# Per-head norms summed on all channels, the power on 256 columns, and the transposed update on all four quarters of TensorE

## The reference, cut to what matters

```python
kk = (k * k_k).astype(jnp.float32).reshape(B, S, H, N)
kk = kk / jnp.maximum(jnp.sqrt(jnp.sum(kk * kk, axis=-1, keepdims=True)), 1e-12)
...
y = wkv7_scan(rh, decay, kh, vh, -kk, kk * ah)
mu = jnp.mean(y, axis=-1, keepdims=True)
var = jnp.mean(jnp.square(y - mu), axis=-1, keepdims=True)
yn = ((y - mu) * lax.rsqrt(var + RWKV_GN_EPS)).reshape(B, S, RW)
```

## Time and profile before

| | |
|---|---|
| median of 3 runs | 1863.61 us (1862.12 to 1864.73) |
| the profiled execution | 1873.29 us, of which the span of its instructions 1871.5 us |
| TensorE matmul busy | 1844.7 us (99%) |
| TensorE weight load busy | 1570.5 us (84%) |
| VectorE, ScalarE, GpSimd busy | 1181.7, 1029.5, 89.4 us |
| mean granted TensorE clock | 0.992 |

### The profile page before, as it was taken

The page is one execution under the profiler, slowest core; times in us unless marked ns, Lnnn a source line. Parts: engine busy times, 40 slices in busy tenths (PEclk is TensorE's granted clock), DMA queues, the critical chain, the costliest instruction groups (busy, mean ns, idle before and its releaser), DMA issues.

```text
span 1871.5 us, 31118 instructions
## 1 busy us (share of the span) xinstructions
PE 1844.7 (99%) x12714; PEld 1570.5 (84%) x12714; DVE 1181.7 (63%) x2432; ACT 1029.5 (55%) x2127; POOL 89.4 (5%) x186
## 2 busy tenths in 40 slices
PE   8999999999999999999999999999999999999998
PEld 7888888888787888888888887888888888878887
DVE  5666545767655567665766664667566767566565
ACT  5565555644433555555655665556455656655554
POOL 0000000211210000010001000000000000000000
PEclk9999999999979999999999999999999999999999
DMA  6555443222214456535652333556355623334552
GB/s 245 181 204 234 160 156 113 103 86 73 97 53 161 136 191 227 201 113 186 238 194 85 133 134 113 189 211 231 112 184 209 235 98 133 136 113 169 202 186 107
DMA packets 42718, 296.30 MB, mean 158 GB/s; under 512 B 4832, under 2 KB 4960, under 8 KB 10576
## 3 DMA queue, kind: packets, MB, share of 16 engines
q1 hardware_dynamic: 41184, 288.48, 43.1%
q0 software_dynamic: 1392, 5.83, 0.9%
HBM read 293.25 MB, written 1.05 MB: 157 GB/s over the span
## 4 chain that ended last, share of the span: by engine, by line
PE 91%; DVE 4%; ACT 3%; DMA 1%; issue 1%; POOL 1%; SPq 0%; POOLq 0%; DVEq 0%; ACTq 0%
PE PS L1865 22%; PE PS L1807 16%; PE PS L1809 15%; PE PS L1808 15%; PE PS L1867 11%; PE PS L1816 1%; PE PS L2108 1%; DVE wlo L2742 1%; PE PS L2310 1%; PE PS L1842 1%; PE PS L2222 1%; PE PS L2089 1%; PE PS L2274 1%; PE PS L2266 1%; PE PS L2101 1%
## 5 line engine op out<-in xcount | busy, mean ns | idle before, releaser
L2742 DVE TENSOR_TENSOR wlo<-raw,whi 128x512 fp32r<-128x512 f32 (+5 forms) x788 | 612.4, 823 | 191.4 <-ACT whi L2353 184.6
L1865 PE MATMUL PS<-xhl,whi 128*128 128x512 f32 x1728 | 612.6, 398 | 0.0
L2353 ACT ACTIVATE whi<-raw 128x512 fp32r<-128x512 f32 (+5 forms) x788 | 531.6, 731 | 140.1 <-PE PS L1809 140.0
L1867 PE MATMUL PS<-xhl,wlo 128*128 128x256 f32 x1728 | 484.7, 280 | 0.0
L1865 PEld LDWEIGHTS PS<-xhl,whi 128*128 128x128 f32 x1728 | 324.6, 188 | 78.9
L1867 PEld LDWEIGHTS PS<-xhl,wlo 128*128 128x128 f32 x1728 | 326.2, 189 | 2.1
L1807 PE MATMUL PS<-whi,yh 128*128 128x512 f32 (+2 forms) x572 | 225.8, 395 | 0.4 <-DVE yl L3127 0.3
L1808 PE MATMUL PS<-wlo,yh 128*128 128x512 f32 (+2 forms) x572 | 222.4, 389 | 0.0
L1809 PE MATMUL PS<-whi,yl 128*128 128x512 f32 (+2 forms) x572 | 222.4, 389 | 0.0
L1807 PE MATMUL PS<-whi,xhl 128*128 128x512 f32 (+4 forms) x480 | 191.4, 399 | 0.3 <-DVE wlo L2742 0.3
L2827 DVE TENSOR_TENSOR arena<-arena,PS 128x256 f32<-128x256 f32 x216 | 90.3, 418 | 159.1 <-ACT arena L2423 159.1
(11 more groups left out here) (268 smaller groups left out, 2405.4 us busy)
## 6 DMA issues: line engine op xcount, KB each, us to landing
raw<-wall SPq DMA_DIRECT2D x249, 1024.0 KB, 4.8
raw<-wall SPq DMA_DIRECT2D x12, 768.0 KB, 4.2
raw<-wall SPq DMA_DIRECT2D x8, 968.0 KB, 4.7
raw<-wall SPq DMA_DIRECT2D x4, 896.0 KB, 4.5
arena<-ebias POOLq DMA_DIRECT2D x2, 768.0 KB, 5.1
raw<-wall SPq DMA_DIRECT2D x2, 720.0 KB, 4.2
raw<-wall SPq DMA_DIRECT2D x2, 640.0 KB, 3.7
X<-x SPq DMA_DIRECT2D x2, 512.0 KB, 6.1
```

The costliest lines, as they stand in the source:

```text
L1865: e.matmul(b, hi[:, c0:c0 + 128], xhl[:, k, :, :].rearrange("p a t -> p (a t)"), start=(k == 0), stop=False, skip_group_check=True)
L1867: p = e.matmul(b[:, 0:256], lo[:, c0:c0 + 128], xh[:, k, :], start=False, stop=(k == 7), skip_group_check=True)
L2353: e.activation(whi[slot_of(i)][:, c].bitcast(F32R), raw[i % 3][:, c], copy).then_inc(*M.sig("whi", ("split", i, q)))
L2742: e.tensor_tensor(wlo[slot_of(i)][:, c], raw[i % 3][:, c], whi[slot_of(i)][:, c].bitcast(F32), ALU.subtract).then_inc(*M.sig("wlo", *[("ha ...
```

## The change

The two norms are summed with the block matrix `bones` (ones where two channels are of one head) as the stationary operand and the squares moving. Every channel of a head then holds its head's sum for every row: 256 columns instead of 4. VectorE's maximum (or scale and offset) and GpSimd's power run on 256 columns, and VectorE's products read the result from SBUF. The spread on ScalarE (`r_key`, `r_wide2`) and the transposes on TensorE (`r_wide`, `r_turn2`) are gone, with their banks. In `r_d` the transpose's update writes to `ps`, in the same two neighbouring banks as the matrix's; one signal tells of both, and VectorE adds the transpose in three instructions, one of 128 partitions and two of 64 that cross the halves. `DENSE` has the second pair of gates ahead of the last streams, `PACE` has new times, `BLANKS` new places; the constants lose two columns.

```diff
-DENSE = (('kvr', 1, 1.0), ('up', 0, 1.0), ('kvr', 2, 1.0), ('kvr', 3, 1.0), ('gate', 2, 1.0), ('gate', 3, 1.0))
+DENSE = (('kvr', 1, 1.0), ('up', 0, 1.0), ('kvr', 2, 1.0), ('gate', 2, 1.0), ('kvr', 3, 1.0), ('gate', 3, 1.0))
...
-    "r_scan": (("dve", 0.62), ("pool", 1.37, "aside")), "r_exp": (("act", 1.04),), "r_nrm": (("dve", 0.08), ("pool", 1.0)),
+    "r_scan": (("dve", 0.62), ("pool", 1.37, "aside")), "r_exp": (("act", 1.04),), "r_nrm": (("dve", 0.36), ("pool", 2.5)),
...
-    ('r_vb', 1, 0): 14, ('r_d', 1, 4, 1): 7, ('r_dm0', 1, 5): 6, ('r_s', 1, 4, 3): 4, ('r_g0', 1, 7): 9,
-    ('r_d', 1, 7, 4): 5, ('r_d', 1, 7, 5): 4, ('r_s', 1, 7, 1): 4, ('r_s', 1, 7, 2): 3, ('r_s', 1, 7, 3): 3,
-    ('r_mean', 1, 7): 4, ('r_var', 1, 7): 7, ('r_turn2', 1, 7): 6, ('wout', 1, 3, 1, 0): 19,
-    ('turn_merged', 1, 4, 0): 4, ('wo', 1, 1, 0, 1): 7, ('proj', 4, 'gh', 0, 0): 20, ('turn_x', 5, 0, 0): 4,
+    ('r_vb', 1, 0): 19, ('r_vb', 1, 2): 7, ('r_yp', 1, 0): 5, ('r_x', 1, 3, 1): 6, ('r_dm0', 1, 4): 4,
+    ('r_dm0', 1, 5): 7, ('r_g0', 1, 7): 10, ('r_s', 1, 6, 3): 3, ('r_var', 1, 6): 3, ('r_s', 1, 7, 1): 4,
+    ('r_s', 1, 7, 2): 3, ('r_s', 1, 7, 3): 3, ('wout', 1, 3, 0, 0): 8, ('wout', 1, 3, 1, 0): 35,
+    ('turn_merged', 1, 4, 0): 4, ('wo', 1, 1, 0, 1): 3, ('wo', 1, 3, 0, 0): 7, ('proj', 4, 'gh', 0, 0): 20,
...
             def r_norm(s, g):
                 for t in due(bank_free(("r_norm", g)), ("act", ("sq", g))):
                     e.wait_ge(*t)
-                head_sums(bank(("r_norm", g)), FR[slot("front", g)].sq).then_inc(*M.sig("pe", ("norm", g)))
-
-            def r_wide(s, g):
-                for t in due(bank_free(("r_wide", g)), ("act", ("wide", g))):
-                    e.wait_ge(*t)
-                turn(bank(("r_wide", g)), 0, FR[slot("front", g)].wide).then_inc(*M.sig("pe", ("wide", g)))
+                e.matmul(bank(("r_norm", g))[:, 0:256], con("bones"), FR[slot("front", g)].sq, start=True, stop=True
+                         ).then_inc(*M.sig("pe", ("norm", g)))
...
-                if k < 5:
-                    b = both("Dd", g, k)
-                    for t in due(*both_free("Dd", g, k), ("dve", ("Xc", g, k))):
-                        e.wait_ge(*t)
-                    for hh, tt, u, ps, cs in units():
-                        p = e.matmul(PS[ps, b[tt], hh * 32:hh * 32 + 32], W_.DT[cs, u, :], some(X[cs, u, :], k, 0),
-                                     start=True, stop=True)
-                    p.then_inc(*M.sig("pe", ("Dd", g, k)))
-                b = bank(("Dt", g, k))
-                for t in due(bank_free(("Dt", g, k)), ("dve", ("Xc", g, k))):
-                    e.wait_ge(*t)
+                b = both("r_d", g, k)
+                for t in due(*both_free("r_d", g, k), ("dve", ("Xc", g, k))):
+                    e.wait_ge(*t)
+                for hh, tt, u, ps, cs in units() if k < 5 else ():
+                    e.matmul(PS[ps, b[tt], hh * 32:hh * 32 + 32], W_.DT[cs, u, :], some(X[cs, u, :], k, 0),
+                             start=True, stop=True)
                 for hh, tt, u, ps, cs in units():
-                    p = e.matmul(b[cs, u * 32:(u + 1) * 32], X[cs, u, :], some(W_.DT[cs, u, :], k, 1),
+                    p = e.matmul(PS[ps, b[tt], 64 + hh * 32:96 + hh * 32], X[cs, u, :], some(W_.DT[cs, u, :], k, 1),
                                  start=True, stop=True)
                 p.then_inc(*M.sig("pe", ("Dt", g, k)))
...
-                o = some(W_.DT, k, 1)
-                for t in due(("pe", ("Dt", g, k))):
-                    e.wait_ge(*t)
-                e.tensor_tensor(o, o, packed(u2(bank(("Dt", g, k))[:, 0:128]), k), ALU.add).then_inc(
-                    *M.sig("dve", ("DT", g, k), ("free", ("Dt", g, k))))
+                    e.tensor_tensor(o, o, packed(b[:, :, 0:64], k), ALU.add).then_inc(*M.sig("dve", ("Dm", g, k)))
+                o = odd(W_.DT[:, 0:2, :], k)
+                e.tensor_tensor(o, o, packed(u2(b[:, 0, 64:128]), k), ALU.add).then_inc(
+                    *M.sig("dve", ("DT", g, k), ("free", ("r_d", g, k, 0))))
+                for q in range(2):
+                    ps, cs = slice(64 * q, 64 * q + 64), slice(64 - 64 * q, 128 - 64 * q)
+                    o = odd(W_.DT[cs, 2:4, :], k)
+                    e.tensor_tensor(o, o, packed(u2(b[ps, 1, 64:128]), k), ALU.add).then_inc(
+                        *M.sig("dve", ("DT", g, k), *[("free", ("r_d", g, k, 1))] * q))
...
-                nrm = FR[slot("front", g)].st
+                nrm = FR[slot("front", g)].wide
                 for t in due(("dve", ("nrm", g)), CST):
                     e.wait_ge(*t)
-                e.tensor_tensor(nrm, nrm, half.to_broadcast([128, 4]), ALU.pow).then_inc(*M.sig("pool", ("nrm", g)))
+                e.tensor_tensor(nrm, nrm, half.to_broadcast([128, 256]), ALU.pow).then_inc(*M.sig("pool", ("nrm", g)))
```

More of the change, by code:

```diff
@@ L1142, in group @@
             yield from self.after(("exp", g))
-            yield from self.room(1)
-            one("r_wide", g)
-            yield 1
             self.do("r_scaled", s, g, 0)
-            free("r_wide", g)
             self.did("bt", g)
@@ L1180, in group @@
                 yield 1
-                while not (len(self.bank.free) >= 3 and self.bank.neighbours() is not None or k == 5 and self.bank.free):
-                    yield 1
-                if k < 5:
-                    self.bank.take_two(*[("Dd", g, k, tt) for tt in range(2)])
-                self.bank.take(("Dt", g, k))
+                yield from self.room_for_two()
+                self.bank.take_two(*[("r_d", g, k, tt) for tt in range(2)])
                 self.do("r_d", s, g, k)
@@ L1191, in group @@
                 splits(g, 2 * (k == 5))
-                if k < 5:
-                    for tt in range(2):
-                        self.bank.give(("Dd", g, k, tt))
-                self.bank.give(("Dt", g, k))
+                for tt in range(2):
+                    self.bank.give(("r_d", g, k, tt))
                 yield 1
@@ L1238, in group @@
             yield 1
-            self.do("r_wide2", s, g)
-            yield 1
-            yield from self.room(1)
-            one("r_turn2", g)
-            yield 1
             yield from self.after(("lg", g))
             self.do("r_fin", s, g)
-            free("r_turn2", g)
             free("r_lg", g)
@@ L1991, in r_lora @@
                 p.then_inc(*M.sig("pe", ("lora", g)))
-            def head_sums(b, src):
-                for tt in range(2):
-                    p = e.matmul(b[:, tt * 2:tt * 2 + 2], src[:, tt * 128:(tt + 1) * 128], con("hsel"), start=True,
-                                 stop=True)
-                return p
             def turn(b, c0, src):
@@ L2179, in r_var @@
                     e.wait_ge(*t)
-                head_sums(bank(("r_var", g)), WH[slot("whole", g)].K).then_inc(*M.sig("pe", ("var", g)))
+                e.matmul(bank(("r_var", g))[:, 0:256], con("bones"), WH[slot("whole", g)].K, start=True, stop=True
+                         ).then_inc(*M.sig("pe", ("var", g)))
             def r_lg(s, g):
@@ L2188, in r_lg @@
                 p.then_inc(*M.sig("pe", ("lg", g)))
-            def r_turn2(s, g):
-                for t in due(bank_free(("r_turn2", g)), ("act", ("wide2", g))):
-                    e.wait_ge(*t)
-                turn(bank(("r_turn2", g)), 0, WH[slot("whole", g)].B).then_inc(*M.sig("pe", ("wide2", g)))
             def lat_turn(s, i, k):
@@ L2576, in r_w @@
                     *M.sig("act", ("w", g), *freed("r_w", g)))
-            def r_key(s, g):
-                F_ = FR[slot("front", g)]
-                for t in due(("pool", ("nrm", g))):
-                    e.wait_ge(*t)
-                e.activation(u4(F_.wide), F_.st.unsqueeze(2).to_broadcast([128, 4, 64]), copy).then_inc(
-                    *M.sig("act", ("wide", g)))
             def r_st(s, g, c):
@@ L2590, in r_st @@
                              scale=W_.st[:, 24 + c:25 + c]).then_inc(*M.sig("act", ("ST", g, c)))
-            def r_wide2(s, g):
-                W_ = WH[slot("whole", g)]
-                for t in due(("pool", ("rsd", g))):
-                    e.wait_ge(*t)
-                e.activation(u4(W_.B), W_.st[:, 4:8].unsqueeze(2).to_broadcast([128, 4, 64]), copy).then_inc(
-                    *M.sig("act", ("wide2", g)))
             def r_ys(s, g):
@@ L2978, in r_nrm @@
                     e.wait_ge(*t)
-                e.tensor_scalar(FR[slot("front", g)].st, bank(("r_norm", g))[:, 0:4], 1e-24, None, ALU.max).then_inc(
+                e.tensor_scalar(FR[slot("front", g)].wide, bank(("r_norm", g))[:, 0:256], 1e-24, None, ALU.max).then_inc(
                     *M.sig("dve", ("nrm", g), ("free", ("r_norm", g))))
@@ L2994, in r_scaled @@
                     return r_scaled_r(g, F_, AR, r3)
[L2995 removed]
+                for t in due(("pool", ("nrm", g))):
                     e.wait_ge(*t)
[L2997 to L2998 removed]
```

(6 more changed lines are left out.)

46 lines of the change are left out of this document (19 added, 27 removed).

## The result

The changed kernel takes **2477.5 us** (median; 2476.8 to 2478.3) against 1862.9 us (1861.6 to 1864.7) of the kernel before on the same chip: ratio 1.329, 95% interval 1.328 to 1.331, so 614.7 us slower. The range of the prediction ended at 1869. Where the forecast put 2.5 us for GpSimd's power on 256 columns, it takes 41.3 us. The profiled execution took 2476.9 us.

A forecast was written before the change was run, and what follows sets the result against it. TensorE, busy 99% of the span, was taken to bound the kernel. From a base of 1863.1 us (median 1863.6), stretches of -5.3, 0 and about +0.5 gave about -5: 1858.6 us, own range 1854 to 1862.5, overall 1850 to 1869.

The forecast's parts named there:

- the cost of GpSimd's power: In both norms, GpSimd's power on 256 columns was put at 2.5 us, +1.4 us a power, +22 us on its queue.
- bounds of 1.17, 2.2 and 50.6 us: GpSimd's 256-column power: width free, 1.17; with the plain operation's width cost, 2.2; growth from one to four columns continued, 50.6.
- Rival 4: GpSimd's wide power is dear: near 1863.6 + 590 at 50.6 us each, 1869 at 6 us; decides from about 4; chance 0.07.
- The work taken off TensorE: Recurrence: transposed update 7.8 us less over 40 blocks, the 16 norms 2 us less; about 9.8 us together.
- the first stretch: Recurrence from 330 to 512.8 us, dense products and group chains sharing TensorE, taken as the limit; balance -5.3 us.
- Rival 1: TensorE's saved time comes back as waits, since whole slots and group order set group 7's end: 1863.5 us, chance 0.20.
- the longer chain: A group's chain: +2 us from the inversion steps, about 1 us longer in all, counting up to three times where uncovered.
- The order of `DENSE`: Later gates in the dense work were said to change no work, group 6 getting its whole slot at 486: nothing.
- The base: The sum starts from 1863.1 us, the profiled 1873.3 less 10.2 for a half-clock stretch that timed runs mostly lack.
- Rival 2: After the last gates, small products and longer waits bring a new half-clock stretch of 20.4 us: 1868.8 us, chance 0.13.
- Rival 3: More comes off: timed runs have the slow stretch and lose it, or group 7's bank wait goes: 1849 us, chance 0.10.

## Why the prediction was wrong

**The step that failed** is the cost of GpSimd's power. The prediction had bounds of 1.17, 2.2 and 50.6 us and took 2.5, from the planner's entry, since other entries follow the trace. An entry for a step that the trace doesn't hold is no measurement, and here it was short by 38.8 us. The rows had the answer: from one column to four the power grew by 0.196 us a column, while the plain operation grew by (1.28 - 0.27) / 255 = 0.004. The width's price of another operation was put on the power although the power's own price stood beside it, some fifty times as high. The measured slope is 0.159, and the upper bound was 9 us too high, the lower two 39 too low.

**Rival 4** was what happened, with a chance of 0.07. Its point of decision, about 4 us, was about right: at 3.7 us the time is 7.6 us above that of a product, and three in a row would be 3 x 3.0 = 9.0. Its price was near (+590 against +614.7), but partly by luck: it took 50.6 us a power and subtracted the stage, as if GpSimd's queue were the limit. The 810 us less 250 are 560; the 590 come out if GpSimd's other steps of the stage, some 30 us, are added. With the true 41.3 the same sum gives 690 - 250 = 440. The queue isn't what limits, for GpSimd itself stands idle in 162 of the stage's 851.7 us: 16 powers hold all engines for 37 to 40 us each, and little other work runs beside them.

**The work taken off TensorE** was right. The transposed update takes 17.7 / 40 = 0.44 us a block in the kernel without powers, where 0.48 was forecast. The product with `bones` costs 4.8 / 8 = 0.60 us, forecast 0.63. VectorE's wide scale takes 0.42 us as forecast, and its adds 17.6 + 8.6 - 11.4 = 14.8 us more, forecast 14.2; its busy time in the stage is 185.4, forecast 182.

**What they are worth** was wrong too, by a few us. Without powers the change brings 1.6 us by the medians, hardly told from none, where 5 were forecast with a dearer power. Were the power 2.5 us long, an estimate between the runs with 0.74 and 3.7 us is 1861.3 + 7.6 x (2.5 - 0.74) / 3.0 = 1866, which would be no change or slower, not faster. The sum gave each microsecond that TensorE saves in the first stretch to the end: -5.3 us up to the end of the dense work, about nothing behind it. The last dense product (`xhl`), in the kernel before and in the one without powers:

```profile
512.44 0.40 PE L1809 MATMUL PS<-whi,xhl 128*128 128x512 f32 x1
```

```profile
514.55 0.40 PE L1792 MATMUL PS<-whi,xhl 128*128 128x512 f32 x1
```

It comes 2.1 us later, not 5 earlier: from 330 to 512.8 us TensorE is idle for 7.5 us without powers, where it was idle for 2.8. What that profiled execution gains, 4 us at the end of the last group (566.9 against the 571.0 us of the kernel with one signal), it gains behind the dense work. Across the runs the end of the last group moves by -4 to +14 us with edits after which the planner weaves differently, as much as any term or more. That is near Rival 1 in mechanism, but larger and of both signs.

**The shared signal and the longer chain**: the signal costs nothing (ratio 1.0006). The quarters' part as a whole costs 4.8 us. The three adds in place of one, on the way to the next step, are the side on which the prediction had +2 a group, under dense work for most groups; that they are what costs was not shown, and part of it is the half clock above. **The order of `DENSE`** was put at nothing and costs 15.9 us alone. **The base** held.

**Rivals 2 and 3.** With all parts and no powers only 3.4 us are at half clock, so a long slow stretch (Rival 2) did not come with the change itself, but it came with two of its parts alone. Nothing like Rival 3's 1849 us was seen; the lowest execution of any of these kernels took 1859.0.

The Trainium skill, "GPSIMD Engine Reference", section 3.1, counts about 2.6 cycles per element for a two-input operation, from which the prediction had an estimate of 1.7 us. The product lies somewhat below that: (612 - 185) / 255 = 1.67 ns a column, 2.0 cycles at the 1.2 GHz that the Trainium skill uses in that section. The power lies far above: 159 ns a column are 191 such cycles. The measurement decides; the case measured in that section of the Trainium skill is an add, and it says nothing of a power.

## What to carry to other kernels

Price a new shape of an operation by the same operation's own rows at other shapes, however small, before any other operation's and before a planner's table; if the own slope gives a bound that would ruin the change, measure that one instruction first. Where every engine follows an order fixed before the run, a step that takes some microseconds longer than planned is paid by all engines, once for each time it runs. And in such a kernel the parts of a change can't be valued one by one, since each edit rearranges the rest: here three parts that lose 5 to 16 us alone are level with the kernel before when they come together.

## What the runs showed of the hardware

GpSimd's power costs 0.16 us for each column, on 16 partitions as on 128, with one exponent for all or one for each element (10.5 us for 64 columns); a product of 256 columns takes 0.61 us. So a power on GpSimd wants its numbers on partitions and few columns, as the kernel before had them: 128 partitions x 4 columns in 1.0 to 1.2 us do what 256 columns do in 41.
